# Delta tiles of a two-block layer: the product of keys and state formed before the inverse instead of after it

## What is computed

```
t_inv = inverse(I + strict_lower(k_beta @ k^T * decay))
u     = t_inv @ (v * beta)
w     = t_inv @ (k_beta * exp(g))
v_new = u - w @ S
o     = q_dec @ S + intra @ v_new
S     = S * g_last + k_dec^T @ v_new
```

## Time and profile before

| | |
|---|---|
| three runs | 1227.77, 1225.25, 1227.01 us; median 1227.01 |
| profiled execution | 1227.18 us, its span 1225.4 us |
| TensorE busy | 1186.3 us, 97% of the span |
| GpSimd busy | 678.1 us, 55% |
| VectorE busy | 638.0 us, 52% |
| ScalarE busy | 315.8 us, 26% |
| mean granted clock of TensorE | 0.99 of full speed |

### The profile page before, as it was taken

How to read it: one execution, slowest core, us unless ns; L and a number is a source line. 1 busy time by engine, 2 the same in 40 slices (tenths; PEclk the granted TensorE clock), 3 DMA queues, 4 the chain that set the end, 5 groups by cost and what they waited for, 6 DMA issues and landing times.

```text
span 1225.4 us, 18867 instructions
## 1 busy us (share of the span) xinstructions
PE 1186.3 (97%) x6848; PEld 976.9 (80%) x6848; DVE 638.0 (52%) x1222; ACT 315.8 (26%) x668; POOL 678.1 (55%) x610
## 2 busy tenths in 40 slices
PE   7999999998998999999899999999999999999997
PEld 6777778777877877877788888878888888888885
DVE  3887554687823575553876657571453300335022
ACT  3125122124631323211235444410221100113001
POOL 4885343444536586765633333366576666666662
PEclk9999999999999999999999999999999999999998
DMA  7231111114013222224521111122333333233321
GB/s 247 87 86 52 53 52 52 53 53 121 2 36 99 81 86 86 69 78 142 203 69 52 37 52 52 53 69 87 90 98 103 89 101 103 86 103 106 100 86 69
DMA packets 29684, 102.41 MB, mean 84 GB/s; under 512 B 3632, under 2 KB 6064, under 8 KB 28848
## 3 DMA queue, kind: packets, MB, share of 16 engines
q1 hardware_dynamic: 27232, 93.47, 24.7%
q10 hardware_dynamic: 2384, 7.99, 2.0%
HBM read 95.16 MB, written 2.10 MB: 79 GB/s over the span
## 4 chain that ended last, share of the span: by engine, by line
PE 84%; DVE 7%; POOL 4%; issue 2%; ACT 2%; DMA 1%; SPq 0%; DVEq 0%; POOLq 0%; ACTq 0%
PE acc L281 23%; PE acc L282 22%; PE acc L283 22%; POOL w_lo L1552 3%; PE aux L494 3%; PE aux L1627 3%; PE aux L484 2%; PE aux L348 1%; PE aux L1609 1%; PE aux L876 1%; PE aux L877 1%; DMA residual<-x 1%; PE aux L789 1%; DVE conv_sum L1962 1%; PE acc L494 0%
## 5 line engine op out<-in xcount | busy, mean ns | idle before, releaser
L1544 POOL CAST w_hi<-w_raw 128x1024 fp32r<-128x1024 f32 x164 | 178.0, 1085 | 497.1 <-issue 358.6
L1552 POOL TENSOR_TENSOR w_lo<-w_raw,w_hi 128x256 fp32r<-128x256 f32 x352 | 292.3, 860 | 7.1
L281 PE MATMUL acc<-ht_hi,w_hi 128*128 128x512 f32 x672 | 271.9, 405 | 6.1 <-DVE ht_lo L392 2.3
L283 PE MATMUL acc<-ht_hi,w_lo 128*128 128x512 f32 x672 | 263.9, 393 | 0.0
L282 PE MATMUL acc<-ht_lo,w_hi 128*128 128x512 f32 x672 | 263.7, 392 | 0.0
L1547 POOL TENSOR_TENSOR w_lo<-w_raw,w_hi 128x1024 fp32r<-128x1024 f32 x76 | 188.0, 2473 | 6.1
L281 PEld LDWEIGHTS acc<-ht_hi,w_hi 128*128 128x128 f32 x672 | 126.9, 189 | 36.7 <-POOL w_lo L1552 6.0
L283 PEld LDWEIGHTS acc<-ht_hi,w_lo 128*128 128x128 f32 x672 | 127.1, 189 | 27.5
L282 PEld LDWEIGHTS acc<-ht_lo,w_hi 128*128 128x128 f32 x672 | 127.4, 190 | 23.8 <-issue 0.7
L281 PE MATMUL acc<-w_hi,ht_hi 128*128 128x512 f32 x256 | 105.9, 414 | 0.3
L281 PE MATMUL acc<-w_hi,ff_hi 128*128 128x512 f32 x256 | 100.4, 392 | 2.3 <-POOL w_lo L1547 2.3
(11 more groups left out here) (425 smaller groups left out, 1928.3 us busy)
## 6 DMA issues: line engine op xcount, KB each, us to landing
w_raw<-units SPq DMA_DIRECT2D x164, 512.0 KB, 3.5
cmp_w<-w_kv ACTq DMA_DIRECT2D x4, 1024.0 KB, 6.8
residual<-x SPq DMA_DIRECT2D x4, 512.0 KB, 7.0
k_turned<-k_split SPq DMA_DIRECT2D x8, 256.0 KB, 3.7
result<-normalized SPq DMA_DIRECT2D x4, 512.0 KB, 2.6
consts_sb<-consts SPq DMA_DIRECT2D x1, 1120.5 KB, 7.0
k_turned<-k_split ACTq DMA_DIRECT2D x2, 512.0 KB, 6.1
norm_post_sb<-norm_post ACTq DMA_DIRECT2D x1, 512.0 KB, 6.0
```

Source lines behind the costliest of these rows:

```text
L281: nc.tensor.matmul(bank, ah, bh, start=start, stop=False)
L283: return nc.tensor.matmul(bank, al, bh, start=False, stop=stop)
L1544: nc.gpsimd.tensor_copy(w_hi[:, slot], raw[:, j]).then_inc(hi_split, 1)
L1552: done = nc.gpsimd.tensor_tensor(w_lo[:, slot, kk, cols], raw[:, j, kk, cols], w_hi[:, slot, kk, cols].bitcast(F32), ALU.subtract)
```

## The change

Since `v_new = t_inv @ (v * beta) - (t_inv @ kbg) @ S`, it can be written `t_inv @ (v * beta - kbg @ S)`. The changed kernel forms keys times S (four products of 128 x 128 x 128) into bank aux[0] in level 0, in the place of a half piece; VectorE scales them behind level 1 (KBG now holds this) and subtracts them from VB behind level 3; KDEC moves from behind level 1 to behind level 0. Behind the inverse one product per head is left, U with VB; WN, ScalarE's negated copy and the semaphores around it are gone. The half piece of level 0 goes to the fill before `solved`; the fills behind it are joined to one of three pieces. One copy of a bias table on ScalarE moves from level 0 to level 1 of tile 3.

```diff
@@ new_values_on_tensor
             for h in range(HG):
-                nc.tensor.matmul(aux[1][:, h * P:(h + 1) * P], G["U"][:, h], G["VB"][:, h],
-                                 start=True, stop=False)
-                done = nc.tensor.matmul(aux[1][:, h * P:(h + 1) * P], G["WN"][:, h], G["S"][:, h],
-                                        start=False, stop=True)
+                done = nc.tensor.matmul(aux[1][:, h * P:(h + 1) * P], G["U"][:, h], G["VB"][:, h],
+                                        start=True, stop=True)
@@ delta_tile_on_tensor
                 per_block(aux[1], G[f"MA{(m + 1) % 2}"], G["TB"]).then_inc(on["x_ready"], 1)
-                fill(0.5)
+                if m == 0:
+                    per_head(aux[0], lambda h: G["KT"][:, h], lambda h: G["S"][:, h]).then_inc(on["ks_ready"], 1)
+                else:
+                    fill(0.5)
...
-            fill(0.5)
+            fill(1)
             pe.wait_ge(on["solved"], n + 1)
-            per_head(aux[0], lambda h: G["KBG"][:, h], lambda h: G["U"][:, h]).then_inc(on["wt_ready"], 1)
             if n == NT - 1:
                 fill(3)
-                pe.wait_ge(on["wn_out"], n + 1)
                 return
-            fill(1)
-            pe.wait_ge(on["wn_out"], n + 1)
             new_values_on_tensor(pe, n)
-            fill(2)
+            fill(3)
             output_on_tensor(pe, n, aux[2])
@@ delta_tile_on_scalar
-            act.wait_ge(on["wt_ready"], n + 1)
-            nc.scalar.activation(G["WN"][:], aux[0][:], ACT.Copy, scale=-1.0).then_inc(on["wn_out"], 1)
@@ alibi_beside
-                if m == 0:
+                if m == 1:
@@ delta_tile_on_vector
-                    if m == 0:
-                        step(V.tensor_tensor(G["KBG"][:], KM[:, :, n], spread(c_kbg[:, four], DG), ALU.mult))
-                    if m == 1 and not last:
+                    if m == 0 and not last:
                         step(V.tensor_tensor(G["KDEC"][:], KM[:, :, n], spread(c_kdec[:, four], DG), ALU.mult))
+                    if m == 1:
+                        eng.wait_ge(on["ks_ready"], n + 1)
+                        step(V.tensor_tensor(G["KBG"][:], as_heads(aux[0]), spread(c_kbg[:, four], DG), ALU.mult))
                     if m == 2:
                         step(V.tensor_tensor(G["VB"][:], VM[:, :, n], spread(beta[:, four], DG), ALU.mult))
+                    if m == 3:
+                        step(V.tensor_tensor(G["VB"][:], G["VB"][:], G["KBG"][:], ALU.subtract))
```

More of the change, by code:

```diff
@@ L206, in two_blocks @@
         G["VN"] = sb("gdn_new_values", [P, HG, DG], F32, 204)
-        G["WN"] = G["DEC"]
         g_first = {"MA0": "TG", "MA1": "IB", "XS": "EG", "TB": "TI"}
@@ L580, in two_blocks @@
                  "gate_cols gate_exps gate_done tg_ready row_sums qk_ready e_ready dec_in dec_ready u0 "
-                 "t0 t0_out masked merged x_ready x_out tx_ready solved wt_ready wn_out vn_ready vn_out "
+                 "t0 t0_out masked merged x_ready x_out tx_ready solved ks_ready vn_ready vn_out "
                  "o_ready o_out o_square z_silu mixed_squares post_done go_done ").split()
@@ L2136, in moba_stage @@
                 return V.tensor_tensor(both[other, g], q[own], both[own, g].bitcast(F32), ALU.subtract)
-            for n in step.loop(NT - 2, 20):
+            for n in step.loop(NT - 2, 21):
                 delta_tile_on_vector(n, lambda m: None, lambda n: prepare_tile(n + 1), False)
@@ L2171, in _ @@
             delta_tile_on_vector(NT - 1, beside_last, last_keys, True)
-            eng.wait_ge(on["x_out"], 6 * NT - 4)
+            eng.wait_ge(on["x_out"], 6 * NT - 3)
             def moba_bias(n):
```

## The result

The changed kernel takes 1229.86 us (median of 20 runs, 1228.38 to 1231.60) against 1227.78 us for the kernel before on the same chips (20 runs): ratio 1.0020, 95% interval 1.0014 to 1.0026. By the ratio that is 2.5 us slower (1.7 to 3.2); the medians lie 2.1 us apart. The profiled execution took 1229.65 us (span 1227.8), 2.47 more than the profiled one of before.

What follows compares the result with a forecast made beforehand. TensorE was taken to bound a delta tile, with VectorE level at tile 2's end. The terms -0.96 - 0.96 + 1.2 + 0.45 = -0.27 from the profiled 1227.18 gave 1226.9 us, range 1223.8 to 1229.4.

Steps and rivals of the forecast that it cites:

- TensorE's part of tiles 0 and 1: Tiles 0 and 1: TensorE loses 0.96 us of work per tile and keeps the whole gain, -1.92 us.
- Edits that cost nothing: Dropped negated copy, moved gate products, added subtraction behind level 3, bias-table copy a level later: no gain or cost.
- Tile 2, the cover of VectorE is gone: End of tile 2: VectorE, slowed beside GpSimd's splits, makes tile 3 begin later, +1.2 us, bounds 0 to 2.0.
- The clock at the boundary: Boundary of tiles 2 and 3: the sum charged no clock fall; only a rival did, at 3.0 us.
- a half-speed stretch more: Rival, chance 0.10: idling at the boundary of tiles 2 and 3 drops TensorE to 1.2 GHz, costing 3.0 us: 1229.9.
- Tile 3: Tile 3's levels: VectorE's fuller level 1 slot delays a merge, x group of level 3 waits; +0.45 us with the attention.
- The attention behind it: Attention start: hangs on ScalarE's chain behind the slab; VectorE's lateness fits its 0.89 us slack; length unchanged behind 300 us.
- the rival's full block: Rival, chance 0.13: two-input VectorE operations first wait for a whole GpSimd piece, 0.88 us, in tile 2: 1228.3 us.

Runs made afterwards that it cites:

- nosub_boundary: Changed kernel without GpSimd's subtractions for the two weight units split behind the inverse of tile 2: 1225.88 us, ratio 0.9988 to the kernel before.
- half_moved_before: Kernel before with only the half piece of level 0 moved behind the last step of the inverse: 1230.51 us, ratio 1.0014 to the kernel before.
- keys_after: Changed kernel with tile 3's K copy and first pair's key work moved from behind tile 2's inverse into levels 2 to 4: 1225.22 us, 0.9982.
- keys_all_after: keys_after plus second pair's remainders behind tile 2's inverse, tile 3's query staging a level earlier, third pair's first key work in levels 3 and 4: 1224.75 us, 0.9973.
- nosub_after: Changed kernel without GpSimd's subtractions for six weight units from the end of tile 2 to the attention: 1225.07 us, ratio 0.9977 to the kernel before.
- nosub_last: Changed kernel without GpSimd's subtractions for the two weight units beside the key work ahead of the attention: 1228.60 us, ratio 1.0012 to the kernel before.
- no_subtraction: Changed kernel without the added VectorE subtraction, so values lack the keys times state term: 1229.29 us, ratio 1.0018 to the kernel before.
- the full rearrangement: The edit of keys_all_after, key and query work of tiles 2 and 3 rearranged on the changed kernel: 1224.75 us, ratio 0.9973 to the kernel before.

## Why the prediction was wrong

It forecast no measurable change with 0.72; the result is slower by 0.20%, past the range by 0.5 us. The sum of the prediction was -0.27, the profiled executions differ by +2.47. The 2.74 between them, step by step. Most of the prediction's signs of being right came: tiles 0 and 1 shorter by 0.96 and 0.85, a wait of 2.45 us for VectorE's output scaling, the fourth split 1.13 us earlier, the remainders over 2 us. One of its signs of being wrong came too: a clock of 0.51 at 251 us.

- **TensorE's part of tiles 0 and 1: right.** The tiles changed by -0.96 and -0.85, forecast was -0.96 for each. The junctions of the new group cost 0.20 and not 0.15.
- **Edits that cost nothing: right.** Leaving out the added subtraction gives nothing that shows, and the product that now reads PSUM takes 0.68 beside GpSimd (270.62, with GpSimd's subtractions from 269.68).
- **Tile 2, the cover of VectorE is gone: the mechanism right, its size too small.** +1.68 for +1.2, inside its bounds of 0 to 2.0. VectorE's stretch grew by 1.99. The overlap with the third split cost 0.84 (both products of IB) for the 0.4 to 0.7 charged, that with the fourth 1.56 (remainders and a product) for 0.7 to 1.3. The price of 0.25 us per us was the mean of a product of 1.10 and one of 0.77. But of the five two-input products beside GpSimd's subtractions four took 1.11 or 1.12 for 0.69, and the one of 0.77, the first behind the sign change, takes 0.76 in nosub_boundary too, where only the end of a cast lies beside it and no subtraction: it never showed their price. Each split also lasted 5.4 us for the 4.9 charged. nosub_boundary measures the whole step with what hangs on it: 3.9 us (2.6 to 5.2).
- **The clock at the boundary: the failed step.** The sum puts the time that TensorE loses behind its new wait at nothing. The loss stood only as the rival "a half-speed stretch more", at 0.10, and put off by the condition that the wait needs another beside it. The wait of 2.45 us stood alone, and the profile has 1.2 GHz for 3.4 us behind it, +1.61, the largest single error of the sum. The rival charged 3.0, twice as much. What the prediction held against the rival, a clock of 1.00 beside a half idle TensorE near 105 us, was one profile's luck: in six of the 14 profiles (half_moved_before, keys_after, keys_all_after, nosub_after, nosub_boundary, nosub_last) TensorE works at 1.2 GHz for 3.4 us between 105 and 110 us, though no edit touches what comes before tile 0. The fall at the boundary is no certain thing either: with the same 2.45 us the clock held in the profile of no_subtraction, and nosub_last again shows the fall. How often it falls there, and what it costs in the median, no run shows.
- **Tile 3: right within 0.2.** +0.23 up to the new values for +0.45. The x group of level 3 waits 0.61 us for the merge, where about 1 was expected.
- **The attention behind it: +1.24 for nothing; VectorE's delay was too small, but what it costs isn't shown.** The prediction hung the start of the attention on ScalarE's chain and gave VectorE a slack of 0.89 and a delay of 0.7 plus up to 0.8. ScalarE's copy of the new values did follow the slab (+1.74, no more than what lay before it). But the key work grew by 2.1 us, since both of GpSimd's splits moved under it and casts lose as well (the second pair 0.88 to 2.07; the first took 1.72 before too), so the output scaling came 2.95 later, 1.2 more than ScalarE's copy. From the copy to the first flip the kernel after takes 1.24 us more. But no_subtraction, whose output scaling is just as late and which has the 6.8 us at 1.2 GHz of the kernel before, takes 51.60, and nosub_boundary, just as late with 3.4 us at 1.2 GHz, takes 51.70; the kernel before took 51.58. The kernels with 13.7 us at 1.2 GHz take 52.7 to 53.7 whether VectorE is late or not (half_moved_before 52.71 with VectorE at 2.8 us). In these profiles the 1.24 goes with the clock, not with VectorE, and nosub_last bounds VectorE's part at 1.0 +-1.7 us.

The Trainium skill (SBUF — State Buffer, "Who interferes with whom") says that casts can enter the modes that take both port pairs and then contend with GpSimd. The trace agrees: a pair takes 0.88 alone, and 1.73 and 2.07 beside GpSimd's subtractions. The prediction charged a cast for this in tile 3 only, 1.0 for 0.45. Of the rival's full block the trace shows less beside subtractions: 0.42 us more for a product beside pieces of 1.06 each (4.24 / 4). Beside one of GpSimd's casts it shows nearly the whole: in nosub_boundary a product and a cast of 1.04 us both start at 244.07, and the product takes 1.58 for 0.69.

**What stays open:** how much of the longer stay at 1.2 GHz in the attention comes from the change. The profiles have 3.4 to 20.5 us there, and the runs of one kernel spread over 2 to 7 us. What decides it wasn't found.

## What to carry to other kernels

Before taking work from the engine that looks like the bound, compare the ends of the other engines at each boundary: where the second engine is level (here 0.16 us of slack), the gain becomes a wait, and the wait may cost more than the gain. A clock that held in one profile beside an idle stretch is no evidence that it will hold in the next. Look at what the shift triggers on the third engine: GpSimd's buffers come free at other times, and its work moves beside VectorE operations that it slows. The change pays once the VectorE work behind the inverse is moved into VectorE's idle time first: 2.7 us (1.1 to 4.3) against the kernel before with the same move, and with the full rearrangement 3.3 us against the kernel before as it was. The rearrangement by itself gives nothing that shows.

## What the runs showed of the hardware

- **Contention slows both sides.** GpSimd's four subtractions take 4.24 us beside VectorE's two-input products, 2.99 to 3.47 where there is little of them; VectorE's products take 1.11 for 0.69, a pair of remainders 2.23 to 2.54 for 1.41, a pair of casts 1.72 to 2.07 for 0.88. An operation with one input from PSUM stays at 0.68. A cast of GpSimd (1.04 us) slows a product that starts with it to 1.58.
- **The clock after a wait.** It fell to 1.2 GHz behind waits of 2.20 and 2.45 us inside otherwise saturated stretches, and held behind 0.64 and 1.09, and once behind 2.45. A fall at the boundary cost 1.6 us up to the next mark.
- **The same place falls in one profile and not in the next.** Between 105 and 110 us TensorE works at 1.2 GHz for 3.4 us in six of 14 profiles and at 2.4 GHz in the others; in the attention the time at 1.2 GHz goes from 3.4 to 20.5 us.
